# VectorE's order within a turn of recurrence and attention, in a two-block transformer kernel

## What is computed

```python
mod = jax.nn.silu(c) @ w_ada[l] + b_ada[l]                 # 6 x 1024 values, 24 MB of weights
sh1, sc1, g1, sh2, sc2, g2 = jnp.split(mod[:, None, :], N_MOD, axis=-1)
u = rmsnorm(h, norm1_w[l]) * (1.0 + sc1) + sh1
hq, hf, hi, hg, aq, ak, av = jnp.split(u @ w_in[l], offs, axis=-1)   # seven of width 512
o_hg = hgrn2(hq, hf, hi, hg, lower_bounds[l], hgrn_gnorm_w[l])       # 4 heads of 128
o_da = diff_attention(aq, ak, av, lam, lambda_init, diff_subln_w[l]) # 4 heads, two softmax maps each
mix = jnp.concatenate([o_hg, o_da.astype(o_hg.dtype)], axis=-1) @ w_out[l]
```

## Time and profile before

| | |
|---|---|
| median of 3 runs | 1275.46 us (1275.23 to 1275.46) |
| the profiled execution | 1278.92 us |
| its span, first to last instruction | 1277.4 us |
| TensorE busy | 1244.1 us, 97% |
| VectorE, ScalarE, GpSimd busy | 591.2, 487.5, 79.7 us |
| mean granted TensorE clock, share of full speed | 0.995 |
| HBM read | 347.05 MB |

### The profile page before, as it was taken

One profiled execution on the slowest core, in us unless ns is written; L12 is line 12 of the kernel. 1 busy time (PEld: TensorE's weight loads), 2 busy tenths in 40 slices (PEclk: granted clock), 3 DMA queues, 4 the chain that ended last, 5 costly groups with the idle time before them and its releaser, 6 DMA issues.

```text
span 1277.4 us, 19117 instructions
## 1 busy us (share of the span) xinstructions
PE 1244.1 (97%) x8248; PEld 945.8 (74%) x8248; DVE 591.2 (46%) x955; ACT 487.5 (38%) x744; POOL 79.7 (6%) x83
## 2 busy tenths in 40 slices
PE   8999999999999999999999999999999999989997
PEld 7888898999999989989999999734444344443432
DVE  3575756444555588386665657532121221212111
ACT  3543464434444654555665554421111111111112
POOL 4021000000000122011122000000000000000000
PEclk9999999999999999999999999999999999999999
DMA  9777435755546334455356558989999999999996
GB/s 352 268 262 265 165 100 176 254 193 170 177 155 213 105 132 137 158 192 165 111 191 207 178 180 334 421 364 420 421 420 422 421 421 420 420 421 422 421 420 263
DMA packets 103316, 349.35 MB, mean 273 GB/s; under 512 B 6290, under 2 KB 9792, under 8 KB 79168
## 3 DMA queue, kind: packets, MB, share of 16 engines
q1 hardware_dynamic: 101488, 345.56, 71.2%
q0 software_dynamic: 1568, 2.50, 0.7%
q10 hardware_dynamic: 176, 0.07, 0.0%
HBM read 347.05 MB, written 1.05 MB: 273 GB/s over the span
## 4 chain that ended last, share of the span: by engine, by line
PE 83%; DMA 6%; DVE 5%; ACT 3%; issue 1%; SPq 1%; DVEq 0%; ACTq 0%
PE bank L553 45%; PE bank L955 14%; PE bank L993 7%; PE bank L752 3%; PE bank L474 2%; DMA arena<-in_expert_w_gate 2%; DMA late_weights<-in_expert_w_up 2%; DMA weights<-in_expert_w_up 2%; PE bank L580 2%; PE bank L510 1%; DVE WHL L1445 1%; SPq L2334 1%; PE bank L800 1%; ACT WHL L1013 1%; PE bank L802 1%
## 5 line engine op out<-in xcount | busy, mean ns | idle before, releaser
L553 PE MATMUL bank<-XH,WHL 128*128 128x256 f32 x2928 | 538.1, 284 | 3.5 <-DVE XL L1465 2.2
L553 PEld LDWEIGHTS bank<-XH,WHL 128*128 128x128 f32 x2928 | 460.0, 192 | 7.9 <-issue 4.6
L553 PE MATMUL bank<-XL,WHL 128*128 128x256 f32 x1464 | 414.2, 283 | 0.0
L1445 DVE TENSOR_TENSOR WHL<-weights,WHL 128x1024 fp32r<-128x1024 f32 x223 | 282.8, 1288 | 203.3 <-ACT WHL L1013 203.0
L1013 ACT ACTIVATE WHL<-weights 128x1024 fp32r<-128x1024 f32 x223 | 230.9, 1054 | 195.4 <-PE bank L553 180.8
L553 PEld LDWEIGHTS bank<-XL,WHL 128*128 128x128 f32 x1464 | 281.3, 192 | 0.1
L955 PE MATMUL bank<-arena 128*64 128x512 f32 x476 | 141.0, 595 | 3.4 <-DMA arena<-in_expert_w_gate 3.4
L553 PE MATMUL bank<-WHL,XH 128*128 128x512 f32 x320 | 101.1, 392 | 0.0
L955 PEld LDWEIGHTS bank<-arena 128*64 128x64 f32 x476 | 42.9, 137 | 74.1 <-issue 66.1
L2162 DVE SCALAR_TENSOR_TENSOR y_lo<-bank,small,y_hi 128x512 fp32r<-128x512 f32 x32 | 24.0, 751 | 128.7 <-ACT y_hi L1419 127.9
L993 PE MATMUL bank<-arena,masks 128*64 128x512 f32 x264 | 75.7, 596 | 0.7 <-ACT masks L1411 0.7
(11 more groups left out here) (363 smaller groups left out, 1363.5 us busy)
## 6 DMA issues: line engine op xcount, KB each, us to landing
weights<-in_w_in SPq DMA_DIRECT2D x58, 1024.0 KB, 5.1
arena<-in_expert_w_gate SPq DMA_DIRECT2D x31, 1024.0 KB, 26.0
arena<-in_expert_w_down SPq DMA_DIRECT2D x31, 1024.0 KB, 26.4
arena<-in_expert_w_up SPq DMA_DIRECT2D x28, 1024.0 KB, 25.7
weights<-in_w_ada SPq DMA_DIRECT2D x22, 1024.0 KB, 7.7
weights<-in_expert_w_down SPq DMA_DIRECT2D x16, 1024.0 KB, 26.6
weights<-in_expert_w_gate SPq DMA_DIRECT2D x15, 1024.0 KB, 26.4
weights<-in_expert_w_up SPq DMA_DIRECT2D x14, 1024.0 KB, 26.3
```

The costliest lines, as they stand in the source:

```text
L553: ins = e.matmul(o, l, r, start=first, skip_group_check=True, stop=g.part == g.parts - 1 and k == g.kc - 1 and n == 2)
L1445: e.tensor_tensor(lo, unit_weights(g, u), hi, ALU.subtract).then_inc(S.w_lo, 1)
```

## The change

It touches only the stretch from hq1 to hg in the first block.

1. **Modulation.** The order of loads has `ada4` and `ada5` ahead of aq (they stood behind it), `ada6` and `ada7` ahead of ak, `ada8` and `ada9` ahead of av. TensorE makes the sum of part 4 between the two halves of hq1 and the sum of part 5 in turn -1, and turns part 4 there; before, sum and turn of part 4 + t stood in turn t. Now turn t has the sum of part 6 + t (to t = 3) and turns part 5 + t (to t = 4). ScalarE copies the row of part 4 behind hq1 and that of part 5 in turn -1. VectorE's step of a part moves from behind the recurrence's work in a turn to between `masked` and the exponents.
2. **VectorE's turn.** `decayed` is cut into `exponents` and `queries`. Between them comes the first part of the attention's work for a head (`diff_maps`: bias, maxima). The second part (`diff_weights`) is a lane of its own that begins with turn 5 and stands first in a turn: the weights of head h are made in turn 5 + h, no longer in turn 4 + h. `diff_norms` is the rest, in the turns where it was.
3. **The unread products** (`spin`) in the attention's steps 0 and 1 are gone.
4. For head 1 the two maps are made in the order 1, 0 (bank 7 first).

```diff
-        order = ([..., "hf1", "hq1", "aq", "ada4", "ada5", "ak", "ada6", "ada7", "av",
-                  "ada8", "ada9", "hv", "hg", "wo0", "wo1", "ada10", "ada11", ...]
+        order = ([..., "hf1", "hq1", "ada4", "ada5", "aq", "ada6", "ada7", "ak",
+                  "ada8", "ada9", "av", "hv", "hg", "wo0", "wo1", "ada10", "ada11", ...]
...
+        maps_of = lambda h: (1, 0) if h == 1 else (0, 1)
...
-                        if step == 1:
-                            spin(by["hv"].banks[0], 16)
...
-                        if step == 0:
-                            spin(by["hv"].banks[0], 18)
-                        for m in range(2):
+                        for i, m in enumerate(maps_of(h)):
...
-            run(gemm("hq1"))
+            hq1 = gemm("hq1")
+            next(hq1)
+            ada_sum(4)
+            run(hq1)
             weave([gemm(n) for n in ("aq", "ak", "av", "hv", "hg", "wo0")],
-                  (0, ada(ada_sum, range(4, 10))),
+                  (-1, ada(ada_sum, range(5, 10))),
                   (-1, gated(HG, [(S.hb, 1), by["hq1"].freed[1]], by["hv"].freed[1])),
-                  (0, ada(ada_turn, range(4, 10))), (4, diff()), (9, gated_spread(HG, S.hg_n)))
+                  (-1, ada(ada_turn, range(4, 10))), (4, diff()), (9, gated_spread(HG, S.hg_n)))
...
             run(hq1)
+            ada_row(4)
...
-                  (0, ada(range(4, 10))), (-1, gated(HG)), (4, diff()))
+                  (-1, ada(range(5, 10))), (-1, gated(HG)), (4, diff()))
...
-                decayed(1)
+                exponents(1)
+                queries(1)
+                next(mods, None)
                 yield
                 for li, m in enumerate(LEVELS):
                     masked(li)
+                    if m > 1:
+                        next(mods, None)
                     if li + 2 < len(LEVELS):
-                        decayed(li + 2)
+                        exponents(li + 2)
+                    if m > 1:
+                        next(maps, None)
+                    if li + 2 < len(LEVELS):
+                        queries(li + 2)
...
-                  (-1, gated(HG, [(S.hb, 1), by["hq1"].freed[1]])), (0, ada(range(4, 10))), (4, diff()))
+                  (5, diff_weights()),
+                  (-1, gated(HG, [(S.hb, 1), by["hq1"].freed[1]], ada(range(4, 10)), diff_maps())), (9, diff_norms()))
```

More of the change, by code:

```diff
@@ L359, in build @@
         ADA = [0, 2, 1] + list(range(3, 12))
-        order = (["ada0", "ada2", "hf0", "hq0", "ada1", "ada3", "hf1", "hq1", "aq", "ada4", "ada5", "ak", "ada6", "ada7", "av",
-                  "ada8", "ada9", "hv", "hg", "wo0", "wo1", "ada10", "ada11", "fg0", "fu0", "fg1"]
+        order = (["ada0", "ada2", "hf0", "hq0", "ada1", "ada3", "hf1", "hq1", "ada4", "ada5", "aq", "ada6", "ada7", "ak",
+                  "ada8", "ada9", "av", "hv", "hg", "wo0", "wo1", "ada10", "ada11", "fg0", "fu0", "fg1"]
                  + [g.name for g in G[by["fu1"].unit0 and G.index(by["fu1"]):]])
@@ L655, in diff @@
                             ins.then_inc(S.da_s, 1)
-                            free[6 + m] = (S.da_b, 2 * h + m + 1)
+                            free[6 + m] = (S.da_b, 2 * h + i + 1)
                     if step == HEADS + 1:
@@ L1494, in ada, with gated, exponents @@
                     yield
-            def gated(L, ready):
+            def gated(L, ready, mods=iter(()), maps=iter(())):
                 n = [0]
-                def decayed(li):
+                def exponents(li):
                     m = LEVELS[li]
@@ L1526, in decayed, with queries @@
                                         ALU.subtract).then_inc(L.sub, 1)
+                def queries(li):
+                    m = LEVELS[li]
+                    E, Q, _ = L.lev[li % 2]
+                    half = m // 2
+                    vw = lambda x: x[:, :, :].rearrange("p h (g m) -> p (h g) m", m=m)
                     w.wait_ge(*L.at(L.exp, li))
@@ L1562, in gated, with diff_maps @@
                 yield
-            def diff():
+            def diff_maps():
                 w.wait_ge(S.pcol, 1)
                 e.tensor_scalar(subs, col("subln"), 1.0 - LAMBDA_INIT, None, ALU.mult).then_inc(S.subs, 1)
-                for step in range(HEADS + 4):
-                    if step < HEADS:
-                        h = step
+                for turn in range(HEADS + 4):
+                    if turn >= 4:
+                        h = turn - 4
                         slope = 2.0 ** (-8.0 * (h + 1) / HEADS)
-                        Sh, Wh = dS[h % 2], dW[h % 2]
+                        Sh = dS[h % 2]
                         w.wait_ge(S.d_masks, 2 * 16)
-                        for m in range(2):
-                            w.wait_ge(S.da_s, 2 * h + m + 1)
+                        for i, m in enumerate(maps_of(h)):
+                            w.wait_ge(S.da_s, 2 * h + i + 1)
                             if h >= 2:
@@ L1578, in diff @@
                                                    op0=ALU.mult, op1=ALU.add).then_inc(S.da_b, 1)
-                            w.wait_ge(S.da_b, 2 * h + m + 1)
+                            w.wait_ge(S.da_b, 2 * h + i + 1)
                             for j, (a0, a1) in enumerate(SPAN):
@@ L1584, in diff @@
                         e.tensor_scalar(dst[:, h, 0:4], dst[:, h, 0:4], -1.0, None, ALU.mult).then_inc(S.da_m, 1)
[L1585 to L1599, removed]
+                    yield
@@ new lines, in diff_weights @@
+            def diff_weights():
+                for h in range(HEADS):
+                    Sh, Wh = dS[h % 2], dW[h % 2]
+                    w.wait_ge(S.da_e, 4 * (h + 1))
+                    e.reciprocal(dst[:, h, 8:12], dst[:, h, 4:8]).then_inc(S.da_n, 1)
+                    w.wait_ge(S.da_n, 2 * h + 1)
+                    w.wait_ge(S.lam_v, 5)
+                    e.tensor_scalar(dst[:, h, 10:12], dst[:, h, 10:12], neglam, None, ALU.mult).then_inc(S.da_n, 1)
+                    w.wait_ge(S.da_n, 2 * h + 2)
+                    if h >= 2:
+                        w.wait_ge(S.da_t, h - 1)
+                    for j, (a0, a1) in enumerate(SPAN):
+                        e.tensor_scalar(Wh[:, a0:a1], Sh[0][:, a0:a1], dst[:, h, 8 + j:9 + j], None,
+                                        ALU.mult).then_inc(S.da_w, 1)
+                        w.wait_ge(S.da_w, 4 * h + 2 * j + 1)
+                        e.scalar_tensor_tensor(out=Wh[:, a0:a1], in0=Sh[1][:, a0:a1],
+                                               scalar=dst[:, h, 10 + j:11 + j], in1=Wh[:, a0:a1], op0=ALU.mult,
+                                               op1=ALU.add).then_inc(S.da_w, 1)
+                    yield
@@ L1600, in diff, with diff_norms @@
+            def diff_norms():
+                for step in range(HEADS + 1, HEADS + 4):
                     if step == HEADS + 1:
```

## The result

The changed kernel takes 1295.08 us (1293.67 to 1297.97), the kernel before 1275.46: ratio 1.0142, 95% interval 1.0127 to 1.0157. It is slower, as forecast, but by 19.6 us where 10.7 were forecast, and the time lies above the range.

The account below looks back on a forecast made before the run. TensorE, busy 97% of the span, was taken to bound the kernel. -8.8 + 5.6 + 3.5 + 3.2 + 3.8 = +7.3, with the clock +10.7, on 1275.46 gave 1286.2 us; range 1278.5 to 1290.5.

Parts of the forecast that it names:

- What is taken away: Turns 4 and 5 lose 34 unread products (7.86 us), turns 0 and 7 lose waits of 0.40 and 0.58: -8.8 us.
- The modulation: In the opening, aq's first piece loads late, delaying ScalarE's chain, so TensorE's turn of part 4 waits: +5.6 us.
- Turn 5: Transposes wait for VectorE's weights behind the low parts, +3.5 us; head 1's second map waits for ScalarE's copy, +3.2 us.
- Turn 7: TensorE waits for VectorE's weights, made behind three low parts as in turn 5: +3.8 us.
- The waits together: Over the changed stretch, removed work and new waits sum to +7.3 us before any clock cost.
- The clock: Behind the opening's and turn 5's waits, two stretches of 3.5 us at half speed: +3.4 us.
- my bound: Limits of the clock term: none to four stretches at half speed, 0 to 6.8 us.
- Rival two: The clock falls at turn 7 too, or stays down twice as long: 1288 to 1290 us, chance 0.14.
- The shift at the end: The feed-forward layer starts about 10 us later, and this shift is still there at the end.

Follow-up runs that it names:

- Kernels 2: The changed kernel with the attention's weights made again at the end of their own turn: 1288.68 us, ratio 1.0096 to the kernel before.
- 11: The changed kernel with ScalarE's copy of a head's transposes moved ahead of the recurrence's exponential (heads 0 to 2): 1294.38 us, ratio 1.0133 to the kernel before.
- kernel 1: The changed kernel with 62 unread products added where TensorE waits longest: 1289.52 us, ratio 1.0100 to the kernel before.
- kernel 5: The changed kernel with 34 unread products put into TensorE's waits, as many as the kernel before had: 1286.01 us, ratio 1.0079 to the kernel before.
- 9: The changed kernel with old modulation order, weights in their own turn, ScalarE's copy before the exponential, and 136 idle TensorE waits: 1272.55 us, ratio 0.9954.
- kernel 10: The changed kernel with 136 idle wait instructions added to TensorE's program and nothing else: 1291.52 us, ratio 1.0118 to the kernel before.
- kernel 7: The kernel before with only VectorE's new order within a turn, old modulation order and the 34 unread products kept: 1286.13 us, ratio 1.0071.
- kernels 3: The changed kernel with the modulation's loads, sums, rows and turns as before, VectorE's step staying at its new place: 1287.67 us, ratio 1.0081.

## Why the prediction was right in kind and wrong in size

**What is taken away** (-8.8). The 34 products and both old waits are gone. Right, as a term.

**The modulation** (+5.6). Right: 5.21 us, by the chain as worked out. Less the opening's 2.7 us the sigmoid was due at 60.7 and stood at 60.46.

**Turn 5** (+3.5 and +3.2). Right: 3.37 us ahead of the transposes. For the second map the list of waits shows only 1.42 us, since at half clock the transposes and the first map fill the rest; the distance is the measure: from the transposes' start to the second map's it was forecast from +11.0 to +15.1, 4.1 us, and is 140.46 - 136.58 = 3.9. Kernels 2 and 11 show that the two have the causes named, low parts and copy.

**Turn 7** (+3.8). Right: 3.80. Turns 6 and 8 have no wait.

**The waits together.** Forecast +7.3; kernel 1, where they cost no clock, measures 8.3 for the stretch. The 1.0 us between was not traced further.

**The clock** (+3.4): the step that failed, as a term mis-sized. I took two stretches of 3.5 us, from the shorter row, and kept the row of 7 us for a rival. Measured were 6.8, 10.2 and 6.8 us, one behind turn 7 as well, costing 7.2 us in place of 3.4; even my bound, four short ones, gave 6.8. Rival two had the mechanism (turn 7 too, longer) but not its full price.

**The end of the program**, the second step that failed: not in the sum at all, and +3.1 us. The prediction stopped at the change's stretch plus what it shifts. Kernels 5, 9 and 10 show that the program's length decides it; that the 3.1 us are a fetch is argued, not shown. Nothing in the profile of before names it; that its last instruction is a taken branch could be read in the kernel, its price only in a trace where the branch is long. Without it the time would still lie above the range: kernel 10, with the short branch, took 1291.52 us, and the range ended at 1290.5.

**The sum of what is explained.** For the median, 8.3 + 7.2 + 3.1 - 1.4 = 17.2 of 19.6 us. The profiled run, at 1293.67, is 18.2 above the median of before, so 1.0 us stays open there; the other 1.4 us are the distance from the profiled run to the median of four runs, of which no other was profiled. The ratio of 1.0142 makes the whole 18.1 us.

**The shift at the end.** It was kept up to the third norm, as forecast, less 0.9 there and 0.5 behind. The experts' loads took nothing back.

## What to carry to other kernels

Unread products in a kernel that waits are not waste to be deleted, but a sign of a wait: move the work that they cover first (here ScalarE's copy and VectorE's modulation step), and then they can go. The waits of TensorE cost here about half their length again through the clock (7.2 us for 13.8), so an order is judged by how its waits are spread as much as by their sum. And after any change to the number of instructions look at what stands behind the last work: here a branch there cost or gave 3 us that had nothing to do with what was changed.

## What was unexpected of the hardware

The granted clock stayed at 0.51 for 6.8 to 10.2 us behind waits of 3.4 to 5.2 us, though TensorE was busy for 8.40 of 10.20 us in turn 5, with a second wait of 1.42 us among them. Its length did not follow the wait's: behind the same 3.8 us of turn 7 it was 6.8 us in the changed kernel and in kernel 7, and 10.2 in kernels 3 and 11. In kernel 5, waits of 1.49, 1.05 and 1.93 us in turns 5 and 7 were followed by full clock, and one of 2.31 us in the opening by 3.4 us at half. The same taken branch took 0.37 us in six programs and 3.37 to 3.61 in seven; 96 more instructions ahead of it, which do nothing, brought it from 3.49 to 0.37.
